# Masked scores times values as split float32r products, in the linear attention of a two-block kernel

## The reference

```
scores = jnp.einsum('nbhik,nbhjk->nbhij', q_dec, k_dec)
scores = jnp.where(causal, scores, 0.0)
o_intra = jnp.einsum('nbhij,nbhjv->nbhiv', scores, vc)
...
o = o_intra + o_inter
```

## Time and profile before

| what | us |
|---|---|
| median of 3 runs | 2684.76 |
| lowest and highest run | 2684.09, 2685.12 |
| profiled execution, its own time | 2684.53 |
| span of the profiled execution | 2682.8 |
| TensorE busy | 2669.4 (100%) |
| VectorE busy | 1709.0 (64%) |
| ScalarE busy | 1263.4 (47%) |

### The profile page before, as it was taken

How to read it: one execution, slowest core, us unless ns; L and a number is a source line. 1 busy time by engine, 2 the same in 40 slices (tenths; PEclk the granted TensorE clock), 3 DMA queues, 4 the chain that set the end, 5 groups by cost and what they waited for, 6 DMA issues and landing times.

```text
span 2682.8 us, 39176 instructions
## 1 busy us (share of the span) xinstructions
PE 2669.4 (100%) x14486; PEld 2315.1 (86%) x14486; DVE 1709.0 (64%) x1853; ACT 1263.4 (47%) x1322; POOL 26.6 (1%) x41
## 2 busy tenths in 40 slices
PE   9999999999999999999999999999999999999998
PEld 8888888888888888888888888888788888888887
DVE  7646666655577555555555668788677764577755
ACT  6544444344444444444444555545554444444443
POOL 0000000000021000000000000000000000000000
PEclk9999999999999999999999999999999999999999
DMA  6555455455555555555554564444545555555553
GB/s 249 188 188 175 172 186 188 172 191 191 183 188 189 188 188 193 182 202 189 188 189 170 182 210 163 158 145 142 204 159 188 187 210 188 196 188 188 188 191 139
DMA packets 74955, 494.55 MB, mean 184 GB/s; under 512 B 8583, under 2 KB 9512, under 8 KB 22072
## 3 DMA queue, kind: packets, MB, share of 16 engines
q1 hardware_dynamic: 74872, 493.42, 53.1%
HBM read 491.29 MB, written 2.10 MB: 184 GB/s over the span
## 4 chain that ended last, share of the span: by engine, by line
PE 97%; DVE 1%; ACT 1%; DMA 0%; issue 0%; SPq 0%; DVEq 0%; ACTq 0%
PE acc L1913 46%; PE acc L1921 24%; PE acc L1967 7%; PE acc L2047 6%; PE acc L1973 4%; PE acc L2052 3%; PE acc L2193 1%; PE aux L2275 1%; PE aux L2340 1%; PE acc L2013 0%; ACT w_hi L617 0%; PE aux L2079 0%; PE acc L2200 0%; PE acc L1941 0%; PE aux L2305 0%
## 5 line engine op out<-in xcount | busy, mean ns | idle before, releaser
L1118 DVE TENSOR_TENSOR w_lo<-raw,w_hi 128x2048 fp32r<-128x2048 f32 (+2 forms) x483 | 1050.4, 2176 | 403.8 <-ACT w_hi L617 358.0
L617 ACT ACTIVATE w_hi<-raw 128x2048 fp32r<-128x2048 f32 (+2 forms) x483 | 879.6, 1821 | 868.7 <-PE acc L1913 497.2
L1913 PE MATMUL acc<-xa,w_hi 128*128 128x512 f32 x4544 | 1090.3, 392 | 0.6 <-DVE xa L1360 0.3
L1913 PEld LDWEIGHTS acc<-xa,w_hi 128*128 128x128 f32 x4544 | 836.3, 188 | 168.6 <-issue 4.2
L1921 PEld LDWEIGHTS acc<-xa,w_lo 128*128 128x128 f32 x4544 | 582.6, 191 | 22.1
L1921 PE MATMUL acc<-xa,w_lo 128*128 128x256 f32 x4544 | 589.4, 283 | 0.0
L1130 DVE TENSOR_TENSOR tmp<-acc,small 128x512 f32<-128x512 f32 x120 | 83.0, 692 | 278.9 <-ACT small L627 278.7
L2047 PE MATMUL acc<-w_hi,xa 128*128 128x512 f32 x768 | 182.4, 390 | 0.0
L1913 PE MATMUL acc<-hid,w_hi 128*128 128x512 f32 x704 | 172.0, 392 | 0.0
L2047 PEld LDWEIGHTS acc<-w_hi,xa 128*128 128x128 f32 x768 | 143.8, 188 | 29.7
L1967 PE MATMUL acc<-w_hi,hid 128*128 128x512 f32 x704 | 167.7, 389 | 0.0
(11 more groups left out here) (334 smaller groups left out, 1611.2 us busy)
## 6 DMA issues: line engine op xcount, KB each, us to landing
raw<-in_w_in SPq DMA_DIRECT2D x158, 1024.0 KB, 5.0
raw<-in_w_gate_up SPq DMA_DIRECT2D x88, 1024.0 KB, 5.0
raw<-in_w_up SPq DMA_DIRECT2D x87, 1024.0 KB, 5.0
raw<-in_w_down SPq DMA_DIRECT2D x64, 704.0 KB, 4.1
raw<-in_w_down SPq DMA_DIRECT2D x40, 1024.0 KB, 4.9
raw<-in_w_out SPq DMA_DIRECT2D x32, 1024.0 KB, 5.0
raw<-in_w_down SPq DMA_DIRECT2D x8, 512.0 KB, 3.5
raw<-in_w_uq SPq DMA_DIRECT2D x3, 1024.0 KB, 4.8
```

The source lines that it names most:

```text
L617: act.activation(hi_part(u, run)[:, 0:kt * P], raw[:, u % RAW, 0:kt * P], ACT.Copy).then_inc(hi_made, splits(u, run))
L1118: dve.tensor_tensor(lo_part(u, run)[:, 0:kt * P], raw[:, u % RAW, 0:kt * P], hi_part(u, run)[:, 0:kt * P], ALU.subtract).then_inc(lo_made, ...
L1913: last = pe.matmul(acc[:, bnk], w_hi[:, u % SPLIT, k * P:(k + 1) * P], x[:, k0 + k], start=first and k == 0, stop=False)
```

## The change

The scores and the values of a head are split like the weights, and the product is done in float32r.

- New tiles: `v_hi`, `v_lo` (128x1024), `sc_hi`, `sc_lo` (128x384), at places in the memory that are free in this stage.
- VectorE, slot 0: makes `v_hi` by a copy, waits for that write, makes `v_lo` by a subtraction.
- ScalarE, slot 1: waits for `masked` and makes `sc_hi` by a copy.
- VectorE, in the second half of the first pair, behind the split of the 5th block: waits for `sc_hi` and makes `sc_lo`.
- TensorE, slot 2: waits for `sc_lo_made` and `v_lo_made` in place of `masked`; for each of the three blocks of scores it multiplies sc_hi with v_hi, sc_lo with v_hi and sc_hi with v_lo, nine products of 512 columns.

```diff
--- before.py
+++ after.py
@@ -217,6 +217,10 @@
+        v_hi = at("v_hi", A + 44 * KB, [P, 2, DV], F32R)
+        v_lo = at("v_lo", A + 48 * KB, [P, 2, DV], F32R)
+        sc_hi = at("sc_hi", A + 52 * KB, [P, 3 * P], F32R)
+        sc_lo = at("sc_lo", A + 57 * KB + 512, [P, 3 * P], F32R)
@@ -345,6 +349,10 @@
+        v_hi_made = sem("v_hi_made")
+        v_lo_made = sem("v_lo_made")
+        sc_hi_made = sem("sc_hi_made")
+        sc_lo_made = sem("sc_lo_made")
@@ -699,6 +707,9 @@
             def head_part(hd, slot):
 
+                if slot == 1:
+                    act.wait_ge(masked, hd + 1)
+                    act.activation(sc_hi[:], sc[:], ACT.Copy).then_inc(sc_hi_made, 1)
                 if slot == 3:
                     act.wait_ge(o_made, hd + 1)
@@ -1248,6 +1259,11 @@
             def head_part(hd, slot, last):
 
+                if slot == 0:
+                    dve.wait_ge(small_made, T_CONV)
+                    dve.tensor_copy(v_hi[:], v_tok[:, bass.ds(hd, 1)]).then_inc(v_hi_made, 1)
+                    dve.wait_ge(v_hi_made, hd + 1)
+                    dve.tensor_tensor(v_lo[:], v_tok[:, bass.ds(hd, 1)], v_hi[:], ALU.subtract).then_inc(v_lo_made, 1)
                 if slot == 1:
                     dve.wait_ge(scores_made, hd + 1)
                     dve.tensor_tensor(sc[:], aux[:, 2, 0:3 * P], mask_s[:], ALU.mult).then_inc(masked, 1)
@@ -1282,6 +1298,9 @@
                     head_part(hd, 2 * p + 1, last)
                     split(u + 4, run)
+                    if p == 0:
+                        dve.wait_ge(sc_hi_made, hd + 1)
+                        dve.tensor_tensor(sc_lo[:], sc[:], sc_hi[:], ALU.subtract).then_inc(sc_lo_made, 1)
                     total(T_CONV + 4 * p + 2, run, 2)
@@ -2079,12 +2098,14 @@
                 if slot == 2:
-                    pe.wait_ge(masked, hd + 1)
+                    pe.wait_ge(sc_lo_made, hd + 1)
+                    pe.wait_ge(v_lo_made, hd + 1)
                     settle()
-                    v = [v_tok[:, bass.ds(hd, 1), c] for c in range(2)]
-                    pe.matmul(aux[:, 0], sc[:, 0:P], v[0], start=True, stop=True)
-                    pe.matmul(aux[:, 1], sc[:, P:2 * P], v[0], start=True, stop=False)
-                    pe.matmul(aux[:, 1], sc[:, 2 * P:3 * P], v[1], start=False, stop=True).then_inc(o_made, 1)
+                    for dst, parts in ((0, ((0, 0),)), (1, ((1, 0), (2, 1)))):
+                        products = [(s, v, n, c) for n, c in parts for s, v in ((sc_hi, v_hi), (sc_lo, v_hi), (sc_hi, v_lo))]
+                        for m, (s, v, n, c) in enumerate(products):
+                            last = pe.matmul(aux[:, dst], s[:, n * P:(n + 1) * P], v[:, c], start=(m == 0), stop=(m == len(products) - 1))
+                    last.then_inc(o_made, 1)
```

## The result

The changed kernel takes 2690.23 us (median of 14 runs, 2689.37 to 2692.43) against 2685.07 us (median of 14 runs of the kernel before): +5.2 us, a ratio of 1.0019 with a 95% interval of 1.0012 to 1.0026. The interval lies wholly above 1, so it is slower, but by just under the 0.2% that the prediction took as its line. The forecast was +5.0 us and 2689.7; of the 0.5 us between, 0.3 is the kernel before, whose median was 2684.76 in the three runs that the forecast started from.

What follows compares the result with a forecast made beforehand. TensorE was taken to bound the kernel. Waits of 6.82 us plus restarts of 0.40 less 2.24 saved on products gave +5.0 us, forecast as 2689.7 us, range 2688.3 to 2691.7.

Steps and rivals of the forecast that it cites:

- What bounds the kernel: Whole program: TensorE, busy 2669.4 of 2682.8 us, sets the end; other engines count only where TensorE waits for them.
- Part 1: TensorE's score-value products: nine float32r products take 2.04 us instead of 2.60, saving 0.56 us a head, 2.24 us in all.
- the mark of 0.1 us: Sign for the products on TensorE: the forecast is wrong if the nine differ from 2.04 us by more than this.
- Part 2: VectorE's split of the values at slot 0: at most 2.64 us, fits a gap of 2.75 us, costed at 0.
- Part 3: Split of the scores on ScalarE and VectorE: 5.30 us from the mask where 3.40 are free; TensorE waits 6.82 us in all.
- the six links: Steps from the mask's end through ScalarE and VectorE to TensorE's first product, added up to 5.30 us in head 0.
- the line of 0.2%: Whole kernel: the change that a measurement tells from none, 5.4 us; slower by more than this was given 0.34.
- The restart: TensorE's start after each wait: about 0.1 us more than a running stream, 0.4 us for four.
- (a): Rival at the wait for the scores: same wait with looser links, 0.29 us more a head, +6.2 us, 2690.9; 30%.
- both overlaps: Early starts before a predecessor's modelled end in the scores' chain: 0.11 us on ScalarE, 0.08 on VectorE.
- (b): Rival at the scores: their split hides, no wait on TensorE, only the products count, -2.2 us, 2682.5; 4%.
- (c): Rival at TensorE's new waits: the clock falls to 1.2 GHz after each, 23 us in all, 2712; 3%.

Runs made afterwards that it cites:

- act_first: Changed kernel with ScalarE's copy into sc_hi moved behind the w_hi of block 4: 2683.01 against 2685.21 us for the kernel before, -2.2 us.
- values3b: Changed kernel with VectorE's subtraction into v_lo done three times, TensorE's own waits left alone: 2690.58 against 2685.47 us for the kernel before, +5.1 us.
- the three reordered kernels: Changed kernel with sc_hi moved behind block 4's w_hi, sc_lo ahead of its w_lo, or both: 2683.01, 2682.96, 2682.84 us; -2.2, -2.3, -2.4 against before.
- wait_alone: Changed kernel with all its splits and waits, but the three old plain float32 products: 2696.74 against 2685.21 us for the kernel before, +11.5 us.
- copies2_look: Second run, for its profile, of the changed kernel with the copy into sc_hi done twice: 2693.97 us in one execution.
- after_again: The changed kernel itself, unedited, measured again beside other runs on one chip: 2690.25 against 2685.47 us for the kernel before, +4.8 us.
- copies9: Changed kernel with nine copies into sc_hi, each waiting for the one before: 2716.8 against 2685.47 us for the kernel before, +31.3 us.
- values3: Changed kernel with the subtraction into v_lo done three times and TensorE's wait count changed to match: 2692.62 against 2685.21 us for the kernel before, +7.4 us.
- copies2: Changed kernel with the copy into sc_hi done twice, the second waiting for the first: 2693.77 against 2685.47 us for the kernel before, +8.3 us.

## Why the prediction was right

**What bounds the kernel: right.** Next to nothing of what the wait cost was given back later. The four blocks account for +5.00 us of the span and the start of the program for 0.7; at TensorE's longest later wait the kernel is 5.64 us behind (1946.79 against 1941.15), at the end of the span 5.6.

**Part 1, the products: right.** Forecast 2.04 us for nine and a saving of 0.56 a head; act_first has blocks 0.56 us shorter in all four heads. The row of the value projection was the right neighbour, and the quarter saved that goes by the Trainium skill's rule of 4 passes (0.65) a little generous. In the changed kernel the nine take 2.14 to 2.16 us with the cost of the restart inside, which by itself would pass the mark of 0.1 us that I had set for being wrong here. Without a wait (act_first) they take 2.07.

**Part 2, the values: right, by a thin margin where it was thin.** The end of head 0 and start of head 1, VectorE, the answer to the earlier trace rows:

```profile
297.39 0.42 DVE L1312 TENSOR_TENSOR qkv<-qkv,tmp 128x256 f32 x1
298.46 0.69 DVE L1264 CAST v_hi<-v_tok 128x1024 fp32r x1 [0.65 <-DVE qkv L1312]
299.19 1.22 DVE L1266 TENSOR_TENSOR v_lo<-v_tok,v_hi 128x1024 fp32r<-128x1024 f32 x1
300.57 2.29 DVE L1129 TENSOR_TENSOR w_lo<-raw,w_hi 128x2048 fp32r<-128x2048 f32 x1 [0.15 <-ACT w_hi L625]
```

The copy took 0.69 us where I had bounded it by 1.22, and 0.65 us passed before it that I hadn't counted: 300.41 - 297.81 = 2.60 us in all, against my 2.64. That the two agree is luck. The next split still waited 0.15 us for ScalarE. values3b shows that the cover behind this gap is at least 2.5 us deeper. By the Trainium skill, page "VectorE: DVE Perf Modes", section "The perf-mode tier table", a float32 copy from SBUF to SBUF runs at twice the rate of a `tensor_tensor`; the trace comes near that, with 0.69 against 1.22 us, 1.8 times.

**Part 3, the scores: right in its path, with luck in the last hundredths.** The delay of TensorE was forecast as 1.90, 1.86, 1.86 and 1.20 us and is 1.91, 1.87, 1.87 and 1.20. Four of the six links are right to 0.02 us, and two miss by more and cancel. VectorE's w_lo starts 0.03 us after the end of w_hi, where I had set 0.11 (218.67 + 1.90 = 220.57, the duration of the first of the two w_hi taken alone, to 220.60). TensorE's first product starts 0.15 us after the end of `sc_lo`, where I had set 0.05. So the chain is 0.10 us shorter than I had it up to the end of `sc_lo` (5.15 us from the mask's end instead of 5.25) and 0.10 us longer behind it: 223.51 - 218.21 = 5.30 us, as forecast. Either miss alone would have moved the time by 0.3 to 0.4 us, the distance between the forecast and the line of 0.2%. The restart costs 0.07 to 0.09 us a head (2.14 to 2.16 against 2.07 us for the nine products), where I had 0.1. What I wrote of the trace was off in one point: the waits are shown as 6.2 us and not 6.8, since the trace counts them from the modelled end.

**The rivals.** (a), looser links, would have been +6.2: both overlaps that it doubted were there (0.10 and 0.08 us). (b) was not what the kernel did, but it is what the three reordered kernels do, at the -2.2 us that it was given. (c) was priced wrong and weighed for the wrong question. I had it as all or nothing, with 5.7 us for each fall, and I took the 1.64 us wait that kept its clock in one profile as a sign that such a wait is safe; in three of the fourteen profiles the clock does fall behind that same wait. What there is: behind the new waits of the changed kernel no fall was seen in its two profiles. One of its 14 executions (2692.43 us) lies 2.2 us above the median, with a mean clock of 0.998. A fall costs 0.4 to 0.5 us behind the 1.64 us wait, 1.6 to 1.7 us a head after a new wait of about 2 us and 2.1 to 2.9 after one of 6. The +5.0 us is the wait itself; the clock adds to the scatter.

## What to carry to other kernels

When an operation is split in two halves on two engines, ask of each half what stands ahead of it in its engine's queue, and what it now holds up itself. Here 1.1 us of work in a place with 3.4 us of room became a chain of 5.3 us. The first half waited for the mask and held up ScalarE's part of a weight split behind it (1.9 us); the second half stood behind VectorE's part of that same split (2.3 us), which needs ScalarE's. Moving either half past its neighbour, a change of three lines, turned +5 us into -2. And a saving of 0.56 us a head is gone with a wait of half a microsecond: compare the gain with the slack before the change is made.

## What the runs showed of the hardware that I had not expected

TensorE's granted clock can fall from the upper level to the lower after idle times of 1.6 to 2.3 us. The fall then comes after work has started again, not in the idle time, by the clock of the stretches within about 1.2 us of the restart (wait_alone: idle 1.92 us, clock 0.72 in the first microsecond of work and 0.52 in the next three; idle 1.87 us, 1.00 for 1.2 us and then 0.50; copies2_look: idle 2.31 us, 0.99 and then 0.50; after_again: idle 1.64 us). After idle times of 5.5 to 6.2 us (copies9) it came inside the idle time, four times in four.

The length of the idle time alone doesn't decide it. 1.92 and 1.87 us brought a fall in heads 0 and 2 of wait_alone, twice in the same place, and 1.87 us in its head 1 brought none. 1.72 to 1.86 us at the same place in the changed kernel, values3 and values3b brought none in any profile. In copies2 and its second look one wait of eight (2.31 us) brought a fall and seven (1.61 to 2.31 us) none. The 1.64 us wait much later in the program brought one in three profiles of fourteen. Whether it is the plain float32 products behind the wait in wait_alone that make the difference, or when in time the wait falls, no run here tells apart.
